# Two norms' gain and offset rows asked for at other moments in a mixture-of-experts decoder step

## Chip, cores and metric

The kernel runs on one core of a Trainium2 chip. The metric is the time of one execution on the device in microseconds (us). The engines are TensorE (PE, matrix products; PEld is its loading of stationary operands), VectorE (DVE), ScalarE (ACT), GpSimd (POOL) and SyncE (SP). SP and POOL each issue transfers from a queue of their own; the profile calls SP's queue q1 and POOL's q0.

## What is computed

One layer over 320 tokens of width 1024: 256 of one prompt and 64 of eight sampled sequences. In the reference's terms:

```python
mod = silu(c) @ w_ada + b_ada            # shift1, scale1, gate1, shift2, scale2, gate2
u = x * (1 + scale1) + shift1
proj = u @ w_in                          # conv branch, pooling branch, two gates
...
h = layer_norm(ALPHA * x + gate1 * (merged @ w_o), ln1_g, ln1_b)
v = h * (1 + scale2) + shift2
f = moe_ffn(v, ...)                      # each token goes to 4 of 32 experts
y = layer_norm(ALPHA * h + gate2 * f, ln2_g, ln2_b)

def expert_block(xb, e):                 # for each of the 32 experts
    h = xb @ w_up[e] + b_up[e]           # 1024 -> 2048
    glu, lin = min(h[:, :1024], 7), clip(h[:, 1024:], -7, 7)
    return (glu * sigmoid(1.702 * glu) * (lin + 1)) @ w_down[e] + b_down[e]
```

All is float32. An expert's weights are 12 MB in float32 (8 MB w_up, 4 MB w_down).

## The kernel before

Everything is written out by hand: each engine has one program, transfers are asked for in a fixed order, and engines wait on semaphores.

**The front.** SP loads weights in chunks of 2 MB into `ring`, which has six slots. The order is: a third of w_ada, the eight parts of w_in, a second third of w_ada, w_out_a, w_out_b, the last third of w_ada, and w_o (two chunks). The product with w_ada gives `mod`, which SP stores to DRAM in thirds (`store_mod`, L391) and reads back as rows copied to all partitions (`mod_for_tokens`, L419 and L421). With them SP loads the rows of the first norm into the ring (L424 and L425). The second third must be in DRAM before these loads are issued (L414). The last third is stored behind them, and when that has landed, scale2 is read back (L428, L429). VectorE waits for those rows, forms the residual and `v` per tile of 128 tokens in the order 0, 2, 1 (`residual`, `gain_and_offset`, `v_rows`). `v` feeds the router, the ranks of the tokens within each expert and the table of rounds.

**The expert loop.** A round handles up to 64 tokens of one expert, and an expert with more takes two rounds; here there are 35 rounds for 32 experts. TensorE does in a round: the up product (L870, four chunks c0 to c3 of 2 MB), small products that combine the last round's result into token order (L844), the gather of the next round's rows (L767), transposes of the activation (L895) and of the next rows (L776), and the down product (L904, four chunks m0 to m3 of 1 MB). Between up and down VectorE does the clamped product twice (`clamp`: L1345, L1346, L1348; `activate`: L1354) with ScalarE's sigmoid (L1035) in between; the transposes wait for both. SP asks for a chunk of the next expert (L437) when TensorE has done with the same chunk of the present one (`expert_used`, L454). SP's waits are in program order, so a late release of m0 holds up all that follows.

**POOL beside it.** POOL first prepares b_up (to L500), waits for the end of the output projection (`wait_full(pool, "o11")`, L502), and loads b_down. At the beginning of round 0 it subtracts parts of `v` (L517, six instructions). Then it asks for the rows of the first norm a second time, into `norm1_rows` (L520, L521), waits for them (L522), and makes the full h of three tiles with them, three instructions per tile (L527, L529, L531), in `hx`. h is used only in the tail. Then it asks for `tail_rows`: gate2 for the prompt (L534), gate2 for eight sequences (L536), ln2_g and ln2_b (L538, L539). After a wait for all of them (L543) POOL sleeps until the last round.

`norm1_rows` lies on the place of `b_up_rows`, which is free after L500. The ln2_g part of `tail_rows` lies on `V`, the ln2_b part on the first half of `norm1_rows`. ln1_g, ln1_b, ln2_g and ln2_b are 512 KB each when copied to 128 partitions.

**The tail.** After the last down product, the last result is combined, and each of three tiles is gated, added to h and normed. POOL multiplies tiles 0 and 1 by ln2_g (L558), adds ln2_b (L560) and stores them; VectorE does tile 2 (L1399, L1400).

Of the kernel before, what the change touches and what calls it, by code (L numbers as in the profile page):

```python
# [16 lines left out]
P = 128  # L17
D = 1024
# [3 lines left out]
NSEQ, TSEQ = 8, 8  # L22
# [6 lines left out]
E = 32  # L29
# [19 lines left out]
EXPERT_CHUNKS = UP_CHUNKS + DOWN_CHUNKS  # L49
# [33 lines left out]
def front_place(name):  # L83
    n = FRONT.index(name)
    return n % 8, n // 8
# [6 lines left out]
def program(nc, a, o):  # L92
    ctx = ExitStack()
    with ctx:
# [3 lines left out]
        def sem(name):  # L98
            return ctx.enter_context(nc.semaphore(name))
# [14 lines left out]
        def region(t, at, *shape):  # L114
            n = int(np.prod(shape))
            v = t[:, at:at + n]
            if len(shape) == 2:
                return v.rearrange("p (a b) -> p a b", a=shape[0])
            if len(shape) == 3:
                return v.rearrange("p (a b c) -> p a b c", a=shape[0], b=shape[1])  # L120
            return v
# [44 lines left out]
        tail_rows = region(front, 0, 4 * D)  # L166
# [7 lines left out]
        norm1_rows = region(front, 3072, 2, D)  # L174
# [58 lines left out]
        expert_landed = [sem(f"expert_landed{c}") for c in range(EXPERT_CHUNKS)]  # L233
# [7 lines left out]
        router_landed = sem("router_landed")  # L241
        norm1_landed = sem("norm1_landed")
        tail_landed = sem("tail_landed")
        bias_landed = sem("bias_landed")
        mod_stored = sem("mod_stored")
        out_stored = sem("out_stored")
# [22 lines left out]
        norm1_again = sem("norm1_again")  # L269
# [8 lines left out]
        b_up_ready = sem("b_up_ready")  # L278
# [63 lines left out]
        def wait_full(eng, name):  # L342
            b, n = front_place(name)
            eng.wait_ge(bank_full[b], n + 1)
            return bank[b]
# [113 lines left out]
        def _(pool):  # L459
# [39 lines left out]
                    part(pool.tensor_copy(parts, rows))  # L499
            pool.memset(b_up_rows[0:1, 0:1], 0.0).then_inc(b_up_ready, 1)  # L500

            wait_full(pool, "o11")  # L502
            for i in range(4):
                pool.dma_start(b_down_raw[32 * i:32 * i + E, :], a["b_down"][0][:, (i // 2) * 512:(i // 2 + 1) * 512]).then_inc(b_down_landed, 16)
# [11 lines left out]
                pool.wait_ge(v_part_ready, PARTS.index((t, q)) + 1)  # L516
                pool.tensor_tensor(V[0:r, t, :], V[0:r, t, :], v_parts[0:r, PART_AT[t][q], :], ALU.subtract).then_inc(v_rest_ready, 1)  # L517

            pool.wait_ge(b_up_ready, 1)
            pool.dma_start(norm1_rows[:, 0, :], a["ln1_g"][0].partition_broadcast(P)).then_inc(norm1_again, 16)  # L520
            pool.dma_start(norm1_rows[:, 1, :], a["ln1_b"][0].partition_broadcast(P)).then_inc(norm1_again, 16)  # L521
            pool.wait_ge(norm1_again, 32)  # L522
            for i, t in enumerate(TILE_ORDER):
                r = ROWS[t]
# [10 lines left out]
            for s in range(NSEQ):  # L535
                pool.dma_start(tail_rows[TSEQ * s:TSEQ * (s + 1), D:2 * D],  # L536
                               mod_rows[1 + s, 5 * D:].partition_broadcast(TSEQ)).then_inc(tail_landed, 16)
            pool.dma_start(tail_rows[:, 2 * D:3 * D], a["ln2_g"][0].partition_broadcast(P)).then_inc(tail_landed, 16)  # L538
            pool.dma_start(tail_rows[:, 3 * D:], a["ln2_b"][0].partition_broadcast(P)).then_inc(tail_landed, 16)  # L539

            pool.wait_ge(table_ready, 1)
            G = pool.value_load(table[0:1, 159:160], min_val=1, max_val=52)
            pool.wait_ge(tail_landed, 16 * (3 + NSEQ))  # L543
            pool.wait_ge(onehot_ready, G + 1)
            pool.wait_ge(bank_full[B_X], G + front_uses(B_X) + 1)
            for i, t in enumerate((1, 2)):
# [8 lines left out]
            for t in range(2):  # L555
                row = out_rows[:, t, :]
                pool.wait_ge(row_normed, 4 + t)
                pool.tensor_tensor(row, row, tail_rows[:, 2 * D:3 * D], ALU.mult).then_inc(h_step, 1)  # L558
                pool.wait_ge(h_step, 7 + 2 * t)
                pool.tensor_tensor(row, row, tail_rows[:, 3 * D:], ALU.add).then_inc(h_step, 1)  # L560
                pool.wait_ge(h_step, 8 + 2 * t)
                pool.dma_start(outs[t], row).then_inc(out_stored, 16)
# [489 lines left out]
        def _(dve):  # L1052
# [5 lines left out]
            def step(ins):  # L1058

                steps[0] += 1  # L1060
                ins.then_inc(step_sem[0], 1)
                dve.wait_ge(step_sem[0], origin[0] + steps[0])

            def signal(ins, sem, value):
                ins.then_inc(sem, 1)
                dve.wait_ge(sem, value)
# [108 lines left out]
            def normalise(r, meanwhile=lambda: None):  # L1175

                step(v.bn_aggr(aggr[0:r, :], stats[0:r, :]))
                normed[0] += 1
                signal(TS(aggr[0:r, 1:2], aggr[0:r, 1:2], EPS, None, ALU.add), var_ready, normed[0])
                meanwhile()  # L1180
                dve.wait_ge(sqrt_ready, normed[0])
                step(v.reciprocal(rstd[0:r, :], rstd[0:r, :]))

                step(STT(rstd2[0:r, :], rstd[0:r, :], rstd[0:r, :], aggr[0:r, 1:2], ALU.mult, ALU.mult))
                step(TS(rstd2[0:r, :], rstd2[0:r, :], -0.5, 1.5, ALU.mult, ALU.add))
                step(TT(rstd[0:r, :], rstd[0:r, :], rstd2[0:r, :], ALU.mult))
                signal(STT(shift[0:r, :], aggr[0:r, 0:1], -1.0, rstd[0:r, :], ALU.mult, ALU.mult), rstd_ready, normed[0])
# [184 lines left out]
                assert steps[0] == PER_LOOP  # L1372
            steps[0], origin[0], step_sem[0] = 0, 0, tail_step

            dve.wait_ge(tail_landed, 16 * (3 + NSEQ))
            dve.wait_ge(h_ready, 3)
            dve.wait_ge(bank_full[B_X], G + front_uses(B_X) + 1)
            gate2 = lambda t, h: tail_rows[0:ROWS[t], (0 if t < 2 else D) + h * 512:(0 if t < 2 else D) + (h + 1) * 512]
# [17 lines left out]
                    normalise(r)  # L1396

            r, row = ROWS[2], out_rows[0:ROWS[2], 2, :]
            normalise(r, meanwhile=lambda: step(STT(row, row, aggr[0:r, 0:1], tail_rows[0:r, 2 * D:3 * D], ALU.subtract, ALU.mult)))  # L1399
            signal(STT(row, row, rstd[0:r, :], tail_rows[0:r, 3 * D:], ALU.mult, ALU.add), y_ready, 1)  # L1400

# [41 lines left out]
```

## Time and profile before

| | |
|---|---|
| three runs | 1304.96, 1297.54, 1305.26 us (median 1304.96) |
| profiled execution | 1306.29 us, of which the span from first to last instruction 1304.5 us |
| mean granted TensorE clock | 0.966 of full speed |
| busy: PE, DVE, ACT, POOL | 1202.6, 550.4, 226.6, 160.6 us |
| DMA | 466.54 MB, mean 358 GB/s |
| expert weights | 128 issues of 2 MB and 128 of 1 MB |

Share of the 16 DMA engines and their rate in 40 slices of 32.6 us:

```profile
DMA  9744499649999999999996999998899999699951
GB/s 335 261 153 173 193 310 369 245 183 400 394 425 428 426 427 427 426 426 425 425 426 255 427 425 426 426 428 356 333 426 428 427 427 426 263 425 426 426 237 40
```

A digit is tenths of the slice, 9 being 90% or more. The expert loop begins in the ninth slice. TensorE is at 9 in nearly all slices as well, but its busy time includes matmuls drawn out behind weights that are arriving, so it does not say by itself which of the two sets the pace.

### The profile page before, as it was taken

The numbers are of one execution on the slowest core, as the hardware profiler recorded it, in microseconds if no ns is written. First come the engines' busy times: TensorE is split into PE (matmuls) and PEld (weight loads), VectorE is DVE, ScalarE is ACT, GpSimd is POOL, SyncE is SP. The second block draws the span as 40 slices with busy tenths as digits, with TensorE's granted clock in tenths as the row PEclk, the third lists the DMA queues.
The fourth block names the chain that finished last, engine by engine and source line by source line (L and its number), as shares of the span: only waits on it lengthen the run. The fifth ranks groups of instructions, "written<-read, shape, count | busy, mean of one in ns | idle before, by whom it ended". The sixth has DMA issues, their size and how long they took to land.

```text
span 1304.5 us, 17407 instructions
## 1 busy us (share of the span) xinstructions
PE 1202.6 (92%) x6170; PEld 520.2 (40%) x6171; DVE 550.4 (42%) x1044; ACT 226.6 (17%) x350; POOL 160.6 (12%) x97
## 2 busy tenths in 40 slices
PE   4899999979899999999899999999999999999990
PEld 0599964433333333333333333333333333333330
DVE  0517825874434333433334333443343433334337
ACT  0233210133112111111111111111111111111110
POOL 0367443024400000000000000000000000000023
PEclk8799999969899999999999999999999999999995
DMA  9744499649999999999996999998899999699951
GB/s 335 261 153 173 193 310 369 245 183 400 394 425 428 426 427 427 426 426 425 425 426 255 427 425 426 426 428 356 333 426 428 427 427 426 263 425 426 426 237 40
DMA packets 54789, 466.54 MB, mean 358 GB/s; under 512 B 5516, under 2 KB 5548, under 8 KB 18642
## 3 DMA queue, kind: packets, MB, share of 16 engines
q1 hardware_dynamic: 52817, 460.32, 85.9%
q0 software_dynamic: 1952, 5.97, 1.4%
q8 instruction: 12, 0.20, 0.1%
q14 instruction: 8, 0.06, 0.0%
HBM read 464.42 MB, written 1.85 MB: 357 GB/s over the span
## 4 chain that ended last, share of the span: by engine, by line
PE 60%; DMA 27%; DVE 9%; SPq 2%; ACT 1%; issue 1%; POOL 0%; DVEq 0%; ACTq 0%
PE bank L870 28%; DMA ring<-in_w_up 21%; PE bank L904 13%; PE bank L647 8%; PE bank L844 3%; DMA mod_rows<-parts_home 3%; DMA hx<-in_x_sample 2%; PE bank L767 2%; PE bank L633 2%; DVE front L1354 1%; PE bank L895 1%; ACT front L1038 1%; DVE front L1348 1%; PE bank L862 1%; DVE front L1345 1%
## 5 line engine op out<-in xcount | busy, mean ns | idle before, releaser
L870 PE MATMUL bank<-ring,front 128*64 128x512 f32 x2240 | 505.9, 597 | 20.3 <-DMA ring<-in_w_up 20.3
L870 PEld LDWEIGHTS bank<-ring,front 128*64 128x64 f32 x2240 | 153.5, 137 | 314.7 <-issue 269.8
L904 PE MATMUL bank<-ring,front 128*64 128x512 f32 x1120 | 250.2, 599 | 7.1 <-ACT front L1038 7.1
L1328 DVE TENSOR_TENSOR front<-front,bank 128x512 f32<-128x512 f32 (+1 forms) x210 | 143.7, 684 | 78.7 <-PE bank L844 65.9
L904 PEld LDWEIGHTS bank<-ring,front 128*64 128x64 f32 x1120 | 77.8, 138 | 155.5 <-issue 141.6
L1371 DVE TENSOR_TENSOR O_low<-bank,O_high 128x512 fp32r<-128x512 f32 x35 | 24.2, 691 | 247.0 <-ACT O_high L1041 247.0
L1035 ACT ACTIVATE front<-front 128x256 f32<-128x256 f32 x70 | 29.2, 417 | 529.0 <-DVE front L1345 529.0
L549 POOL TENSOR_TENSOR parts_home<-front 128x1024 f32<-128x1024 f32 (+1 forms) x2 | 4.7, 2356 | 919.9 <-DVE onehot_T L1368 919.9
L1345 DVE TENSOR_SCALAR front<-bank 128x256 f32<-128x256 f32 x70 | 29.7, 424 | 159.8 <-PE bank L870 158.6
L467 POOL TENSOR_TENSOR ring_parts<-ring,ring_parts 128x1024 fp32r<-128x1024 f32 x28 | 68.3, 2472 | 77.2 <-ACT ring_parts L937 77.2
L767 PE MATMUL bank<-parts_home,front 128*64 128x512 bf16 (+1 forms) x560 | 70.5, 382 | 0.0
L647 PE MATMUL bank<-u_high,ring_parts 128*128 128x320 f32 x448 | 67.1, 308 | 0.0
L844 PE MATMUL bank<-O_high,onehot_T 64*128 64x512 f32 x216 | 54.5, 501 | 13.5 <-DVE front L1390 11.7
L647 PEld LDWEIGHTS bank<-u_high,ring_parts 128*128 128x128 f32 x448 | 66.0, 188 | 0.0
L1041 ACT ACTIVATE O_high<-bank 128x512 fp32r<-128x512 f32 x35 | 20.9, 597 | 236.3 <-PE bank L904 236.3
L1268 DVE TENSOR_TENSOR front<-const,front 128x192 bf16 x35 | 14.8, 423 | 95.3 <-issue 95.3
L767 PEld LDWEIGHTS bank<-parts_home,front 128*64 128x64 bf16 (+1 forms) x560 | 32.3, 109 | 52.7 <-issue 35.3
L844 PEld LDWEIGHTS bank<-O_high,onehot_T 64*128 64x128 f32 x216 | 20.4, 185 | 80.2 <-issue 80.2
L1354 DVE SCALAR_TENSOR_TENSOR front<-front 128x256 f32<-128x256 f32 x70 | 49.8, 712 | 2.5
L1035 ACT ACT_TABLE_LOAD x35 | 44.9, 1283 | 0.6
L844 PE MATMUL bank<-O_low,onehot_T 64*128 64x512 f32 x216 | 43.1, 395 | 0.0
L605 PE MATMUL bank<-ring,small 128*9 128x512 f32 x192 | 27.7, 722 | 15.2 <-DMA ring<-in_w_ada 15.2
(217 smaller groups left out, 938.6 us busy)
## 6 DMA issues: line engine op xcount, KB each, us to landing
ring<-in_w_up SPq DMA_DIRECT2D x128, 2048.0 KB, 18.3
ring<-in_w_down SPq DMA_DIRECT2D x128, 1024.0 KB, 17.4
ring<-in_w_ada SPq DMA_DIRECT2D x12, 2048.0 KB, 16.0
ring<-in_w_in SPq DMA_DIRECT2D x8, 2048.0 KB, 11.9
ring<-in_w_o SPq DMA_DIRECT2D x2, 2048.0 KB, 19.6
hx<-in_x_prompt SPq DMA_DIRECT2D x2, 1024.0 KB, 23.7
ring<-in_w_out_a SPq DMA_DIRECT2D x1, 2048.0 KB, 7.3
ring<-in_w_out_b SPq DMA_DIRECT2D x1, 2048.0 KB, 14.2
```

Of the source, the lines that this page charges most:

```text
L467: pool.tensor_tensor(ring_parts[:, slot, part], ring[:, slot, part], ring_parts[:, HIGH_SLOT[i % 2], part].bitcast(F32), ALU.subtract).the ...
L605: last = mm(ps[32 * q:32 * q + NC_ROWS, :], sc_T[:, k, :], w[:, kk, q * 512:(q + 1) * 512], start=k == 0, stop=k == KC - 1)
L633: last = mm(blocks[j][:, 0:NT], w[:, k, j * P:(j + 1) * P], u_T[:, k, :], start=k == 0, stop=k == KC - 1)
L647: return mm(blocks[j][:, 0:NT], w[:, k, j * P:(j + 1) * P], u[:, k, :], start=start, stop=stop)
L767: last = mm(bank[B_X][64 * h:64 * h + 64, :], S[0:r, t, :], v_parts[0:r, at, h * 512:(h + 1) * 512], start=i == 0, stop=i == len(GATHER) - 1)
L844: last = mm(bank[B_C[h]][:, :], onehot_T[rows, t * P:(t + 1) * P], part[rows, :], start=not stop, stop=stop)
L870: last = mm(bank[B_UP[j]][64 * h:64 * h + 64, :], x_T[:, (c % 2) * 2 + b, 64 * (c // 2):64 * (c // 2) + 64], w[:, :, at:at + 256], start=F ...
L904: last = mm(bank[B_DOWN][64 * h:64 * h + 64, :], act_T[:, 2 * j + b, 64 * hh:64 * hh + 64], expert_chunk_at(UP_CHUNKS + m)[:, b * 1024 + h ...
L1035: AF(sig[:, j, :], glu[:, j, :], ACT.Sigmoid, scale=SWISH).then_inc(sig_ready, 1)
L1328: signal(TT(Y[0:r, 2 * t + h, :], Y[0:r, 2 * t + h, :], bank[b][0:r, :], ALU.add), bank_free[b], value)
L1345: signal(TS(glu[:, j, :], bank[b][:, 0:256], LIMIT, None, ALU.min), glu_ready, 2 * g + j + 1)
L1354: signal(STT(by_row, in_rows(lin), slot_gate, in_rows(sig), ALU.mult, ALU.mult), act_ready, 2 * g + j + 1)
```

## The change

The two loads of the first norm's rows into `norm1_rows` go from behind L517 to behind L500, ahead of POOL's wait for the output projection. Their wait (L522) stays where it was. The two loads of the last norm's rows go behind a new wait, for chunk m3 of the last expert. They signal a new semaphore `norm2_landed`. The two old waits for `tail_landed` count two loads less, and POOL (before its first L558) and VectorE (before the norm of tile 2) wait for `norm2_landed`.

```diff
--- before.py
+++ after.py
@@ -241,6 +241,7 @@
         router_landed = sem("router_landed")
         norm1_landed = sem("norm1_landed")
         tail_landed = sem("tail_landed")
+        norm2_landed = sem("norm2_landed")
         bias_landed = sem("bias_landed")
         mod_stored = sem("mod_stored")
         out_stored = sem("out_stored")
@@ -499,6 +500,9 @@
                     part(pool.tensor_copy(parts, rows))
             pool.memset(b_up_rows[0:1, 0:1], 0.0).then_inc(b_up_ready, 1)
 
+            pool.wait_ge(b_up_ready, 1)
+            pool.dma_start(norm1_rows[:, 0, :], a["ln1_g"][0].partition_broadcast(P)).then_inc(norm1_again, 16)
+            pool.dma_start(norm1_rows[:, 1, :], a["ln1_b"][0].partition_broadcast(P)).then_inc(norm1_again, 16)
             wait_full(pool, "o11")
             for i in range(4):
                 pool.dma_start(b_down_raw[32 * i:32 * i + E, :], a["b_down"][0][:, (i // 2) * 512:(i // 2 + 1) * 512]).then_inc(b_down_landed, 16)
@@ -516,9 +520,6 @@
                 pool.wait_ge(v_part_ready, PARTS.index((t, q)) + 1)
                 pool.tensor_tensor(V[0:r, t, :], V[0:r, t, :], v_parts[0:r, PART_AT[t][q], :], ALU.subtract).then_inc(v_rest_ready, 1)
 
-            pool.wait_ge(b_up_ready, 1)
-            pool.dma_start(norm1_rows[:, 0, :], a["ln1_g"][0].partition_broadcast(P)).then_inc(norm1_again, 16)
-            pool.dma_start(norm1_rows[:, 1, :], a["ln1_b"][0].partition_broadcast(P)).then_inc(norm1_again, 16)
             pool.wait_ge(norm1_again, 32)
             for i, t in enumerate(TILE_ORDER):
                 r = ROWS[t]
@@ -535,12 +536,13 @@
             for s in range(NSEQ):
                 pool.dma_start(tail_rows[TSEQ * s:TSEQ * (s + 1), D:2 * D],
                                mod_rows[1 + s, 5 * D:].partition_broadcast(TSEQ)).then_inc(tail_landed, 16)
-            pool.dma_start(tail_rows[:, 2 * D:3 * D], a["ln2_g"][0].partition_broadcast(P)).then_inc(tail_landed, 16)
-            pool.dma_start(tail_rows[:, 3 * D:], a["ln2_b"][0].partition_broadcast(P)).then_inc(tail_landed, 16)
 
             pool.wait_ge(table_ready, 1)
             G = pool.value_load(table[0:1, 159:160], min_val=1, max_val=52)
-            pool.wait_ge(tail_landed, 16 * (3 + NSEQ))
+            pool.wait_ge(tail_landed, 16 * (1 + NSEQ))
+            pool.wait_ge(expert_landed[EXPERT_CHUNKS - 1], 16 * E)
+            pool.dma_start(tail_rows[:, 2 * D:3 * D], a["ln2_g"][0].partition_broadcast(P)).then_inc(norm2_landed, 16)
+            pool.dma_start(tail_rows[:, 3 * D:], a["ln2_b"][0].partition_broadcast(P)).then_inc(norm2_landed, 16)
             pool.wait_ge(onehot_ready, G + 1)
             pool.wait_ge(bank_full[B_X], G + front_uses(B_X) + 1)
             for i, t in enumerate((1, 2)):
@@ -555,6 +557,8 @@
             for t in range(2):
                 row = out_rows[:, t, :]
                 pool.wait_ge(row_normed, 4 + t)
+                if t == 0:
+                    pool.wait_ge(norm2_landed, 32)
                 pool.tensor_tensor(row, row, tail_rows[:, 2 * D:3 * D], ALU.mult).then_inc(h_step, 1)
                 pool.wait_ge(h_step, 7 + 2 * t)
                 pool.tensor_tensor(row, row, tail_rows[:, 3 * D:], ALU.add).then_inc(h_step, 1)
@@ -1372,7 +1376,7 @@
                 assert steps[0] == PER_LOOP
             steps[0], origin[0], step_sem[0] = 0, 0, tail_step
 
-            dve.wait_ge(tail_landed, 16 * (3 + NSEQ))
+            dve.wait_ge(tail_landed, 16 * (1 + NSEQ))
             dve.wait_ge(h_ready, 3)
             dve.wait_ge(bank_full[B_X], G + front_uses(B_X) + 1)
             gate2 = lambda t, h: tail_rows[0:ROWS[t], (0 if t < 2 else D) + h * 512:(0 if t < 2 else D) + (h + 1) * 512]
@@ -1396,6 +1400,7 @@
                     normalise(r)
 
             r, row = ROWS[2], out_rows[0:ROWS[2], 2, :]
+            dve.wait_ge(norm2_landed, 32)
             normalise(r, meanwhile=lambda: step(STT(row, row, aggr[0:r, 0:1], tail_rows[0:r, 2 * D:3 * D], ALU.subtract, ALU.mult)))
             signal(STT(row, row, rstd[0:r, :], tail_rows[0:r, 3 * D:], ALU.mult, ALU.add), y_ready, 1)
```

## Rows read from the trace of the kernel before

**Rows 1.** The page: the chain of waits that ended last, by engine and by line.

```profile
PE 60%; DMA 27%; DVE 9%; SPq 2%; ACT 1%; issue 1%; POOL 0%; DVEq 0%; ACTq 0%
PE bank L870 28%; DMA ring<-in_w_up 21%; PE bank L904 13%; PE bank L647 8%; PE bank L844 3%; DMA mod_rows<-parts_home 3%; DMA hx<-in_x_sample 2%; PE bank L767 2%; PE bank L633 2%; DVE front L1354 1%; PE bank L895 1%; ACT front L1038 1%; DVE front L1348 1%; PE bank L862 1%; DVE front L1345 1%
```

**Rows 2.** The same chain in order of time: start, us, what.

```profile
216.09 14.36 DMA mod_rows<-parts_home
...
419.97 24.13 DMA ring<-in_w_up
...
654.62 25.65 DMA ring<-in_w_up
```

**Rows 3.** Stretches: us, busy PE, PEld, DVE, ACT, POOL, clock, DMA share, GB/s.

```profile
290.00:300.00 10.00, 10.00 (x50) 3.23 (x48) 4.94 (x8) 6.18 (x6) 10.00 (x6) 1.00 0.70 249
300.00:310.00 10.00, 9.73 (x58) 3.98 (x56) 5.82 (x12) 5.01 (x8) 2.20 (x3) 1.00 0.98 399
310.00:320.00 10.00, 10.00 (x52) 3.38 (x48) 1.18 (x2) 1.88 (x2) 1.29 (x1) 1.00 1.00 419
...
340.00:360.00 20.00, 20.00 (x87) 6.42 (x88) 5.19 (x11) 2.48 (x3) 3.09 (x7) 0.89 1.01 371
...
690.00:700.00 10.00, 10.00 (x52) 3.43 (x50) 1.49 (x3) 1.88 (x2) 0.00 (x0) 1.00 0.03 8
...
1257.00:1258.00 1.00, 1.00 (x8) 0.31 (x6) 0.93 (x3) 0.32 (x1) 0.00 (x0) 1.00 0.50 205
```

**Rows 4.** DMA between 209 and 224 us; then POOL's queue between 293 and 360.

```profile
DMA packets 1408, 5.98 MB, mean 399 GB/s; under 512 B 88, under 2 KB 88, under 8 KB 1268
...
q0 software_dynamic: 883, 2.57, 10.3%
```

**Rows 5.** POOL in order of time: start, us, line, operation, idle before.

```profile
208.72 0.09 POOL L500 MEMSET front<- 1x1 f32 x1
...
301.09 0.56 POOL L520 DMA_DIRECT2D front<-in_ln_g  x1
...
318.71 2.36 POOL L527 TENSOR_TENSOR hx<-hx,front 128x1024 f32<-128x1024 f32 x1 [16.51 <-DMA front<-in_ln_b]
...
330.75 2.36 POOL L527 TENSOR_TENSOR hx<-hx,front 128x1024 f32<-128x1024 f32 x1
```

**Rows 6.** VectorE in order of time, the clamped product of rounds 0 and 1.

```profile
303.60 0.43 DVE L1348 SCALAR_TENSOR_TENSOR front<-front 128x256 f32<-128x256 f32 x1
...
306.18 0.68 DVE L1354 SCALAR_TENSOR_TENSOR front<-front 128x256 f32<-128x256 f32 x1
...
330.77 2.62 DVE L1348 SCALAR_TENSOR_TENSOR front<-front 128x256 f32<-128x256 f32 x1
333.43 2.64 DVE L1354 SCALAR_TENSOR_TENSOR front<-front 128x256 f32<-128x256 f32 x1
```

**Rows 7.** TensorE in order of time, rounds 0 and 1.

```profile
308.26 7.09 PE L904 MATMUL bank<-ring,front 128*64 128x512 f32 x32 [0.21 <-ACT front L1038]
...
338.20 1.11 PE L895 MATMUL bank<-const,front 128*128 128x128 f32 x4 [4.18 <-DVE front L1354]
...
340.10 9.23 PE L904 MATMUL bank<-ring,front 128*64 128x512 f32 x32
```

**Rows 8.** SP's issues in order of time: start, us, what.

```profile
292.23 12.63 SPq L437 DMA_DIRECT2D ring<-in_w_up  x4
310.38 5.48 SPq L437 DMA_DIRECT2D ring<-in_w_down  x4
319.40 12.63 SPq L437 DMA_DIRECT2D ring<-in_w_up  x4
343.96 5.89 SPq L437 DMA_DIRECT2D ring<-in_w_down  x4
```

**Rows 9.** The tail, all engines in order of time.

```profile
1263.03 2.36 POOL L549 TENSOR_TENSOR parts_home<-front 128x1024 f32<-128x1024 f32 x1 [919.94 <-DVE onehot_T L1368]
...
1282.75 2.39 POOL L558 TENSOR_TENSOR parts_home<-parts_home,front 128x1024 f32<-128x1024 f32 x1 [10.19 <-ACT parts_home L969]
```

## The prediction

> **What bounds the kernel now.** The chain of waits comes first [rows 1]. It ends in TensorE for 60% and in DMA for 27%, nearly all of the latter w_up. So the loop has two limits that take turns. The same chain in order of time shows where [rows 2]. From the loop's start to 420 us it runs along TensorE alone. From 419.97 to 680 us it runs through one w_up transfer per round, nine in all, the last of 25.65 us. After that it is mostly TensorE again. There is one such transfer ahead of the loop that matters too: the store of the last third of `mod`, 14.36 us.
>
> The stretches say what the chain can't [rows 3]. DMA is busy without a gap from 293 us on: 0.98 at 300 to 310, 1.00 at 310 to 320, and so in all slices to 680 us. It first stands still at 690 to 700 us (0.03), when an expert takes two rounds. So TensorE lives on chunks loaded ahead up to 444 us, but the moment at which it gets past 680 us was set by the transfers queued since 293 us. A byte taken out of this stream counts, even one at 301 us where TensorE waits for nothing; a gap put into it counts just as much. After 690 us both follow the shift that they had at 680.
>
> **The change part by part.** Experts are numbered from 0, so the first stream is expert 1's.
>
> *The two ln1 loads leave the stream.* They are issued at 301.09 [rows 5] and are 1.05 MB. POOL's queue moved 2.57 MB in 10.3% of 67 us, 6.9 us [rows 4], so 1.05 MB cost 2.8 us. The lower bound is 2.5 us at 419 GB/s. The upper one takes them for the cause of the slowest stretch, 371 instead of 419 GB/s from 340 to 360 us [rows 3]: that is 0.96 MB less, 2.3 us, so 4.8 in all. I take -2.8, as the queue's own rate is the nearest row.
>
> *The two ln2 loads leave the stream.* Same size, same bounds, and they do lie just before that slow stretch. I take -2.8, at most -4.8. Together the two give 5.6.
>
> *The two ln1 loads arrive at 208.8.* POOL is free there since its last memset [rows 5]; b_up_ready is its own signal and costs nothing. But this is not an empty place. Between 209 and 224 us DMA moves 399 GB/s [rows 4] for w_o, for SP's own copies of the ln1 rows and for the rows of `mod`, and behind them waits the store that is on the chain from 216.09 to 230.45 [rows 2]. VectorE's first residual and then scale2 wait for just these, and from there VectorE's serial chain leads to the table and to the loop. 1.05 MB at 399 GB/s are 2.6 us of delay. From below: before, the pair on POOL's queue landed only at 318.7 after an issue at 301.65 [rows 5], 1.05 MB in 17 us or 62 GB/s beside SP's queue. At that pace 0.9 MB come through up to 223 us and the rest falls behind, where the engines are half idle: 2.0 us. Nothing excludes 0 if all of it slid there. From above: 4.8, as for the slow stretch. I take +2.6, as the nearest row is that of the stretch itself.
>
> The Trainium skill, DMA: Bandwidth & Descriptors, section "Queues, rings and completion order", states that each DMA engine takes turns between the queues it has work for, a packet at a time. By that rule the POOL loads can't wait behind SP's, which speaks against this half of the change: the head's term would be the full 2.6, and 0 would be excluded. The trace before agrees in part: the pair did land while SP's queue was full, but only after 17 us, so the turns were not equal in bytes.
>
> *POOL's work on h moves.* Its wait for the rows was 16.51 us [rows 5]. It disappears, so L527 begins behind L517 at 301.1 and the nine instructions end at 319, not 337. In round 1 these had collided with VectorE: L1348 took 2.62 us beside POOL's L527 at 330.75, against 0.43 in round 0, and L1354 2.64 against 0.68 [rows 5, 6]. Each held until POOL's instruction ended. Then TensorE stood idle 4.18 us, and L904 took 9.23 instead of 7.09, the granted clock being 0.89 from 340 to 360 us [rows 3, 7]. Now the same nine meet round 0. On the old time axis L529 runs 303.5 to 305.9, L531 to 307.0, L527 to 309.5, L529 to 312.0. L1348 at 303.60 is held to 306.2; L1354 and two instructions that were not held before follow up to 307.9; the second L1348 is held to 309.8, the second L1354 to 312.3. Without POOL it ended at 306.86 [rows 6]: TensorE waits 5.4 us. Round 1, which lasted 34.0 us between the first L870 and the next against 27.2 in undisturbed rounds, is freed of these 6.8 us and round 0 gets about 8. For TensorE alone that cancels, and up to 444 us its time is not the bound.
>
> For the stream it does not cancel. SP asks for m0 of expert 1 when TensorE has read m0 of expert 0: 310.38 [rows 8], 2.1 us into L904. In the slowed round 1, L904 began 2.0 instead of 1.4 us after the last L1354, and m0 was asked for 3.9 instead of 2.1 us into it [rows 7, 8]. So now it is asked for at 310.38 + 5.4 + 0.6 + 1.7 = 318.1, and with the head's delay at 320.7. What has DMA until then? The four w_up chunks, 8.39 MB, plus ln1, 1.05 MB. 2.49 + 3.99 MB are moved by 310 [rows 3], and the remaining 2.96 MB at 419 GB/s last to 317.1. Before, there were 6.7 us of work in the queue when m0 was asked for at 310.38. Without ln1 the work ends at 314.3, with the head's delay at 316.9. From the issue at 320.7 the data take about 1.4 us (between 0.8 and 1.9, from 292.23 to the first bytes and to a full rate). So DMA stands idle from 316.9 to 322.1: **5.2 us**. A second gap is covered: m0 to m3 last 10 us, to 332.1, with gate2's rows behind them, and c0 of expert 2 is asked for at 319.40 + 2.6 + 8.1 = 330.1 [rows 8]. The bounds are 0, if POOL's instructions don't hold VectorE there, and 7.
>
> *The ln2 loads at the end.* The last chunk has landed by about 1257.7, where DMA falls to half [rows 3]. POOL is asleep until 1263.03 and first uses the rows at 1282.75, 25 us later [rows 9]; VectorE later still. Two issues of 0.56 us and 2.8 us of transfer are covered by that wait: 0. Without the cover they would cost 4 to 5 us. The two added waits for `norm2_landed` are already met. What is queued behind POOL's new wait is only the tail, which it slept through anyway.
>
> **The sum.** +2.6 + 5.2 - 2.8 - 2.8 = +2.2 us. On the profiled execution's 1306.29 us that gives 1308.5. That execution lies 1.3 us above the median of the runs, so I forecast **1307 us**, against 1304.96. A measurement of this kernel can tell about 1% from no change, 13 us; its own three runs lie 7.7 us apart.
>
> **The rivals.** *A, the stream does not run dry.* POOL's work on h meets VectorE less than I have it, or m0 comes early enough; then the 5.2 fall to 0 and the saved bytes stay saved: +2.6 - 5.6 = -3.0, 1302. With a head that costs nothing and ln2 at its 4.8 it is -7.6, 1297. For it: my 6.7 us of queue are worked out from rates of 10 us stretches, and a collision depends on fractions of a microsecond. Against: nine instructions without a gap can't miss a product of four.
>
> *B, slower, the clock.* TensorE stood idle 4.18 us in round 1 and lost 2.1 us in L904 behind it. Behind 5.4 us the clock may stay at the lower of its two levels, 1.2 GHz, for all of L904: twice 7.09, 14.2 instead of 9.2 us. Then m0 comes 1.5 us later, and each of the three chunks behind it is released every 3.5 us where DMA needs 2.5, so it waits 1 us for each. That is +2.2 + 4.5 = +6.7, and with the head at 4.8 +8.9: 1312 to 1314. It becomes a loss over 1% only where the gap reaches 5.2 + 10.8 = 16 us. Against it: in round 1 the idle time was nearly as long, and L904 took 9.23, so the clock came back within it.
>
> *C, the change does nothing of the kind*: the ln rows were never in the way because TensorE, not DMA, sets 680 us. Then the head's 2.6 and the difference of the rounds are left, 5.4 + 0.6 + 2.1 = 8.1 in round 0 less 6.8 in round 1: +3.9, 1309. Rows 2 speak against it.
>
> **How the numbers follow.** Forecast 0.45, A 0.33, B 0.10, C 0.07, others 0.05. The range covers the forecast (1303 to 1311 with its bounds), A and B: 1297 to 1313. That holds 0.95 by the cases; I take off what the scatter of the runs may put outside, and am left with 0.8. No case with the prices above leaves the 1%. I give faster by over 1% 0.03 (before's fastest run, 1297.54, with A gets near 1292), slower by over 1% 0.04 (B with a larger gap), within 1% 0.93.
>
> **What would show it.** In the profile of the changed kernel: the wait of VectorE for the rows of `mod` ends near 232, not 229.7; the loop's first L870 starts 2.6 us later. POOL's L527 starts right behind L517. The long L1348 and L1354 are in round 0, and TensorE's wait of about 5 us for L1354 stands there and not in round 1. DMA shows a gap of some 5 us near 317 to 322. The w_up transfer that ends near 680 ends near 682. At the end two loads stand at 1258 to 1263 and no wait for them. Signs against me would be: no gap in DMA near 320 (then A), a round 0 longer than 38 us (then B), or TensorE waiting for the rows in the tail.

## The result, and the profile after

The changed kernel takes **1308.34 us** (median of 20 runs, 1306.20 to 1311.63) where the kernel before takes 1304.83 (20 runs, 1297.54 to 1309.00). The ratio is 1.003, with a 95% interval of 1.0021 to 1.0040: 2.7 to 5.2 us slower. The forecast was 1307 us, 2.2 above before.

Lines have other numbers in the changed kernel. TensorE's L870 is now L874, L895 is L899 and L904 is L908. VectorE's L1348 and L1354 are L1352 and L1358. POOL's L527, L529 and L531 are L528, L530 and L532, its L558 is L562, and SP's L437 is L438. In ln1_half they are as before; in the other experiments they are up to two higher than in the changed kernel.

The chain of waits in order of time (start, us, what) answers to [rows 2]:

```profile
216.93 14.16 DMA mod_rows<-parts_home
231.11 4.13 DMA ring<-mod_rows
...
449.13 25.64 DMA ring<-in_w_up
...
655.78 25.62 DMA ring<-in_w_up
```

The chain is of the same kind, with eight w_up transfers where before had nine. The last one before DMA's first rest ends at 681.40, 1.1 us later than before's 680.27. DMA sets the time from 449 and not from 420 us on. That fits the start of round 2, which is 1.8 us later on TensorE (351.43 against 349.60) where the stream is 1.1 us later, but no run shows that this is the reason.

The stretches (busy PE, PEld, DVE, ACT, POOL, then granted clock, DMA share, GB/s) answer to [rows 3]:

```profile
290.00:300.00 10.00, 10.00 (x48) 3.17 (x46) 4.94 (x8) 5.28 (x5) 10.00 (x5) 0.95 0.58 210
300.00:310.00 10.00, 8.00 (x46) 2.83 (x42) 5.97 (x7) 4.67 (x6) 9.74 (x6) 1.00 1.00 416
310.00:320.00 10.00, 6.27 (x22) 2.95 (x24) 6.71 (x6) 1.24 (x3) 9.58 (x6) 0.66 0.50 213
320.00:330.00 10.00, 10.00 (x52) 3.37 (x50) 2.31 (x4) 1.88 (x2) 5.07 (x10) 1.00 0.99 357
```

At 310 to 320 us DMA is busy for half the time, where before it was at 1.00. Finer, at each end of the gap:

```profile
314.00:315.00 1.00, 1.00 (x6) 1.00 (x6) 0.88 (x2) 0.12 (x1) 0.92 (x2) 0.50 0.89 377
315.00:316.00 1.00, 1.00 (x6) 0.59 (x6) 0.96 (x2) 0.74 (x2) 1.00 (x1) 0.50 0.16 66
316.00:317.00 1.00, 1.00 (x4) 0.24 (x2) 0.97 (x2) 0.33 (x1) 0.92 (x2) 0.50 0.00 0
...
319.00:320.00 1.00, 1.00 (x6) 0.28 (x4) 0.00 (x0) 0.00 (x0) 0.91 (x2) 1.00 0.00 0
320.00:321.00 1.00, 1.00 (x8) 0.41 (x6) 0.00 (x0) 0.00 (x0) 0.46 (x1) 1.00 0.88 188
```

From about 315.2 to 320.2 nothing moves. The granted clock is at the lower level (0.50) from about 311.5 to 318.3; TensorE had been idle since 308.0, and the clock came back within L908. What made the gap is on three engines. POOL (start, us; it answers to [rows 5]):

```profile
302.22 2.35 POOL L528 TENSOR_TENSOR hx<-hx,front 128x1024 f32<-128x1024 f32 x1
304.65 2.36 POOL L530 TENSOR_TENSOR hx<-hx,front 128x1024 f32<-128x1024 f32 x1
307.11 1.10 POOL L532 TENSOR_SCALAR hx<-hx 128x1024 f32<-128x1024 f32 x1
308.28 2.45 POOL L528 TENSOR_TENSOR hx<-hx,front 64x1024 f32<-64x1024 f32 x1
310.81 2.40 POOL L530 TENSOR_TENSOR hx<-hx,front 64x1024 f32<-64x1024 f32 x1
```

VectorE beside it [rows 6], and TensorE behind it [rows 7]:

```profile
304.74 2.55 DVE L1352 SCALAR_TENSOR_TENSOR front<-front 128x256 f32<-128x256 f32 x1
307.32 1.33 DVE L1358 SCALAR_TENSOR_TENSOR front<-front 128x256 f32<-128x256 f32 x1
...
309.60 1.42 DVE L1352 SCALAR_TENSOR_TENSOR front<-front 128x256 f32<-128x256 f32 x1
311.05 2.62 DVE L1358 SCALAR_TENSOR_TENSOR front<-front 128x256 f32<-128x256 f32 x1
```

```profile
313.73 1.11 PE L899 MATMUL bank<-const,front 128*128 128x128 f32 x4 [5.73 <-DVE front L1358]
...
315.63 8.41 PE L908 MATMUL bank<-ring,front 128*64 128x512 f32 x32
```

Each of VectorE's four instructions ends just behind one of POOL's: 307.29 behind 307.01, 308.65 behind 308.21, 311.02 behind 310.73, 313.67 behind 313.21. TensorE waits 5.73 us for the last. SP then asks for m0 (the first issue of `in_w_down` here) at 319.06 and not at 310.38 [rows 8]:

```profile
293.37 12.63 SPq L438 DMA_DIRECT2D ring<-in_w_up  x4
319.06 5.48 SPq L438 DMA_DIRECT2D ring<-in_w_down  x4
328.09 12.62 SPq L438 DMA_DIRECT2D ring<-in_w_up  x4
```

The tail [rows 9] has the two loads ahead of POOL's gating, and no engine waits for them:

```profile
1261.43 0.55 POOL L544 DMA_DIRECT2D front<-in_ln_g  x1 [935.79 <-DMA ring<-in_w_down]
...
1264.75 2.36 POOL L551 TENSOR_TENSOR parts_home<-front 128x1024 f32<-128x1024 f32 x1 [2.25 <-DVE onehot_T L1372]
...
1284.46 2.40 POOL L562 TENSOR_TENSOR parts_home<-parts_home,front 128x1024 f32<-128x1024 f32 x1 [10.19 <-ACT parts_home L973]
```

### The profile page after: what moved, and what is told of

The parts are those of the page before. It is cut to its first block, busy times and chain, and to the rows that moved or that the text cites. A ratio compares the mean times of both kernels' runs of the same rounds, so it can differ in the third digit from the quotient of the medians.

```text
span 1306.2 us, 17410 instructions
## 1 busy us (share of the span) xinstructions
PE 1201.9 (92%) x6170; PEld 518.7 (40%) x6171; DVE 558.9 (43%) x1044; ACT 226.5 (17%) x350; POOL 160.6 (12%) x97
## 3 DMA queue, kind: packets, MB, share of 16 engines
HBM read 464.42 MB, written 1.85 MB: 357 GB/s over the span
## 4 chain that ended last, share of the span: by engine, by line
PE 64%; DMA 26%; DVE 7%; ACT 1%; issue 1%; SPq 1%; POOL 0%; DVEq 0%; ACTq 0%
PE bank L874 29%; DMA ring<-in_w_up 20%; PE bank L908 14%; PE bank L651 8%; PE bank L848 4%; PE bank L771 3%; DMA ring<-in_w_ada 3%; DMA hx<-in_x_sample 2%; PE bank L637 1%; PE bank L899 1%; ACT front L1042 1%; DMA mod_rows<-parts_home 1%; PE bank L866 1%; PE bank L609 1%; PE bank L833 1%
## 5 line engine op out<-in xcount | busy, mean ns | idle before, releaser
L874 PE MATMUL bank<-ring,front 128*64 128x512 f32 x2240 | 506.1, 597 | 20.1 <-DMA ring<-in_w_up 20.0
L874 PEld LDWEIGHTS bank<-ring,front 128*64 128x64 f32 x2240 | 153.3, 137 | 314.8 <-issue 269.2
L908 PE MATMUL bank<-ring,front 128*64 128x512 f32 x1120 | 249.4, 598 | 7.0 <-ACT front L1042 7.0
L908 PEld LDWEIGHTS bank<-ring,front 128*64 128x64 f32 x1120 | 77.6, 137 | 154.8 <-issue 140.9
L1358 DVE SCALAR_TENSOR_TENSOR front<-front 128x256 f32<-128x256 f32 x70 | 50.3, 719 | 2.5
## 6 DMA issues: line engine op xcount, KB each, us to landing
ring<-in_w_down SPq DMA_DIRECT2D x128, 1024.0 KB, 17.6
```

The lines of the kernel that those rows point to most:

```text
L874: last = mm(bank[B_UP[j]][64 * h:64 * h + 64, :], x_T[:, (c % 2) * 2 + b, 64 * (c // 2):64 * (c // 2) + 64], w[:, :, at:at + 256], start=F ...
L908: last = mm(bank[B_DOWN][64 * h:64 * h + 64, :], act_T[:, 2 * j + b, 64 * hh:64 * hh + 64], expert_chunk_at(UP_CHUNKS + m)[:, b * 1024 + h ...
L1358: signal(STT(by_row, in_rows(lin), slot_gate, in_rows(sig), ALU.mult, ALU.mult), act_ready, 2 * g + j + 1)
```

## Experiments

Every kernel was measured against the kernel before, and each row of the table has one trace. The scatter of a kernel's runs (some 5 us) is larger than most of the terms. The traces split the time into parts, of which the stream and the rest scatter less: in the three kernels that were traced twice, the stream differs by 0.1 to 1.7 us and the rest by 0.3 to 1.3 us. A difference of 1 us between two streams therefore says nothing. The table below is worked out from the traces. "Loop starts" is the start of the first up product. "Stream" is from there to the end of the w_up transfer near 680 us, the last on the chain before DMA's first rest. "Rest" is from there to the issue of the last store. "Against before" is by the ratio of the runs, in us with its 95% interval.

| kernel | loop starts | stream | rest | against before |
|---|---|---|---|---|
| before | 287.04 | 393.2 | 618.4 | |
| changed | 288.14 | 393.3 | 618.9 | +3.9 (2.7 to 5.2) |
| changed_again | 286.01 | 392.7 | 619.8 | +3.0 (1.3 to 4.7) |
| ln1_half | 287.86 | 395.4 | 619.7 | +4.2 (2.2 to 6.1) |
| ln2_half | 286.07 | 390.1 | 619.2 | -3.1 (-4.8 to -1.3) |
| h_held | 287.43 | 387.8 | 618.7 | -3.9 (-5.7 to -2.2) |
| ln1_in_idle_dma | 286.13 | 388.6 | 619.0 | -6.1 (-8.2 to -3.9) |
| ln1_in_idle_dma_again | 285.43 | 386.9 | 618.8 | -5.1 (-6.9 to -3.4) |
| h_round0_no_head | 286.58 | 392.8 | 619.6 | +1.3 (-0.1 to 2.7) |
| h_round0_no_head_again | 285.25 | 392.9 | 618.3 | +1.4 (-0.3 to 3.1) |
| h_in_round_9 | 288.88 | 388.0 | 620.3 | -4.6 (-6.1 to -3.1) |
| all_tail_rows_last | 284.40 | 383.1 | 622.4 | -6.1 (-7.8 to -4.6) |
| gate_rows_beside_last_down | 284.56 | 383.3 | 620.2 | -6.5 (-8.2 to -4.8) |

**The changed kernel beside the others.**

> The changed kernel itself, beside the others. My theory: the stream of expert weights sets the time at 680 us. The head costs +1.3 us (the trace after shows the loop starting 1.1 us later), DMA stands idle for 5.1 us in round 0, the four loads taken out give back 5.6 us: about +1 to +2 us, with the 20 runs so far at +3.5. Rival 'head': the gap is covered by chunks loaded ahead and costs nothing, and what the change costs lies before the loop. Rival 'TensorE': TensorE sets the time, the loads were never in the way, and what is left is that round 0 loses more than round 1 gains. All three have to give this kernel's +2 to +4 us.

Measured: 1308.42 us against 1304.56. Its loop started at 286.01, 2 us sooner than in the first trace, and the stream took the same 393 us. So the start of the loop scatters by itself, and a head term can't be read from it in one trace. The +3.0 (1.3 to 4.7) lies above the +1 to +2 that my theory gave.

In this trace and the four others with the gap, what DMA's share is short of 1.00, summed over the slices of 1 us about the gap, is 4.8 to 5.4 us.

**The ln1 loads alone.** The lines on ln2 are as before. Against the kernel before:

```diff
 # POOL
+            pool.wait_ge(b_up_ready, 1)
+            pool.dma_start(norm1_rows[:, 0, :], ...)      # ln1_g
+            pool.dma_start(norm1_rows[:, 1, :], ...)      # ln1_b
             wait_full(pool, "o11")
 ...
-            pool.wait_ge(b_up_ready, 1)                   # behind L517
-            pool.dma_start(norm1_rows[:, 0, :], ...)
-            pool.dma_start(norm1_rows[:, 1, :], ...)
             pool.wait_ge(norm1_again, 32)
```

> Only the ln1 loads are moved; the ln2 loads stay in the stream behind gate2's rows. My theory: the changed kernel plus the 2.8 us of the ln2 loads, so 2 to 4 us above the changed kernel and about +4 to +6 us against before. Rival 'TensorE': equal to the changed kernel. Rival 'head': the stream matters there too, so the same as my theory; this run does not tell those two apart.

Measured: 1310.47, 2.05 us above the changed kernel's median. Its stream of 395.4 is 2.4 longer than the changed kernel's (mean of two, 393.0). That fits the ln2 pair. "TensorE sets the time" asked for no difference; the intervals of the two kernels overlap, so this run alone doesn't settle it.

**The ln2 loads alone.** Against the changed kernel:

```diff
-            pool.wait_ge(b_up_ready, 1)                   # not ahead of "o11"
-            pool.dma_start(norm1_rows[:, 0, :], ...)
-            pool.dma_start(norm1_rows[:, 1, :], ...)
 ...
+            pool.wait_ge(b_up_ready, 1)                   # behind L517, as before
+            pool.dma_start(norm1_rows[:, 0, :], ...)
+            pool.dma_start(norm1_rows[:, 1, :], ...)
             pool.wait_ge(norm1_again, 32)
```

> Only the ln2 loads are moved; the ln1 loads and POOL's work on h stay where they were. My theory: nothing in the head, no gap, 1.05 MB less in the stream: -2.8 us against before (-2.5 to -4.8). Its trace should show the w_up transfer that ends at 680 us end 3 us earlier, round 1 as slow as before, and the tail unchanged with the two loads behind the last chunk. Rival 'TensorE': 0.

Measured: 1302.85 against 1304.56; the stream is 3.2 us shorter than before's, ending at 650.49 + 25.64:

```profile
650.49 25.64 DMA ring<-in_w_up
```

This half of the change is a gain of 3.1 us by the runs (1.3 to 4.8), where 2.8 was forecast and "TensorE" asked for 0. The loss is in the other half.

**POOL's work held back to round 1.** Against the changed kernel:

```diff
+            pool.wait_ge(O_low_ready, 2)
             pool.wait_ge(norm1_again, 32)
```

> The changed kernel, but POOL's work on h waits until VectorE has the low part of round 0's result (about 317 us), so that it meets VectorE in round 1, as before, and not in round 0. The ln1 loads stay early. My theory: the gap of 5.1 us in DMA goes, and the time falls by about 5 us against the changed kernel, to -2 to -4 us against before; the trace shows DMA without a gap at 315 to 321 us. Rival 'head': equal to the changed kernel. Rival 'TensorE': equal to the changed kernel within 1 us, since one slow round takes the place of another.

Measured: 1301.64, 6.8 us below the changed kernel on the same chip. One added wait on POOL turns the loss into a gain. The gap is nearly gone (clock 0.84, DMA share 0.88 here, against 0.66 and 0.50 in the changed kernel), where I had expected none of it; some 1.3 us are left at 313 to 316 us. In this trace VectorE waited 2.08 us for ScalarE, with POOL idle, and TensorE 1.85 us for VectorE; its down product then began at the lower clock and took 8.68 us and not 7.09:

```profile
310.00:320.00 10.00, 9.98 (x42) 3.34 (x44) 1.39 (x3) 1.69 (x3) 0.00 (x0) 0.84 0.88 328
```

```profile
308.68 0.65 PE L900 MATMUL bank<-const,front 128*128 128x128 f32 x4 [1.85 <-DVE front L1359]
...
310.02 8.68 PE L909 MATMUL bank<-ring,front 128*64 128x512 f32 x32 [0.21 <-ACT front L1043]
```

The rival "head", by which the gap is covered, and the rival "TensorE" both wanted no change. Both fall. That one slow round only took the place of another holds for TensorE: rounds 0 and 1, from the first up product of round 0 to that of round 2, last 62.4 us here and 63.3 and 63.1 us in the two traces of the changed kernel, 0.6 to 0.9 us more, while the stream differs by 5.2.

**The ln1 loads where DMA rests.** As h_held, and against it:

```diff
-            pool.wait_ge(b_up_ready, 1)                   # ahead of "o11"
-            pool.dma_start(norm1_rows[:, 0, :], ...)
-            pool.dma_start(norm1_rows[:, 1, :], ...)
             wait_full(pool, "o11")
 ...
             pool.memset(Y, 0.0).then_inc(cleared, 1)
+            pool.wait_ge(b_up_ready, 1)
+            pool.dma_start(norm1_rows[:, 0, :], ...)
+            pool.dma_start(norm1_rows[:, 1, :], ...)
```

> As h_held, with the ln1 loads issued not at 209 us but behind POOL's clearing of Y at about 280 us, where the trace of before shows DMA at a share of 0.01 (280 to 290). My theory: the head's term, +1.3 us by the trace after (2.6 as predicted), goes: 1 to 3 us below h_held, -4 to -6 us against before. The loads land within 5 us and nothing waits for them. Rival 'the early loads are free in the head': equal to h_held.

> The same kernel as ln1_in_idle_dma, to narrow the size of the gap's cost against the next one: -4 to -6.5 us against before.

Measured: 1299.69 and 1298.65, so -6.1 and -5.1 against before, where h_held had -3.9. The loads landed in 4.7 us, against 17 us for the pair before. DMA is at 1.00 from 310 to 320 us. The intervals of this kernel and h_held overlap, so these runs alone do not show the head's term; the traces do, below.

**The gap without the head.** The changed kernel with the ln1 loads behind the clearing of Y, POOL's work not held.

> The changed kernel with the ln1 loads behind the clearing of Y (about 280 us), and POOL's work on h not held, so in round 0 as in the changed kernel. It has the gap without the head's term. My theory: 1 to 3 us below the changed kernel, so between 0 and +2 us against before, and 5 us above ln1_in_idle_dma. Rival 'head': the same as ln1_in_idle_dma.

> The same kernel as h_round0_no_head. By the gap in its trace (DMA at rest from about 313.5 to 318.5 us) it should be 5 us above ln1_in_idle_dma_again; the first runs had 7.1 between the medians. If the gap is all, the difference is 4 to 6; if something else is lost as well, 6 to 8.

Measured: +1.3 and +1.4 against before, 7.1 and 6.4 us above ln1_in_idle_dma in the two sets of runs. The streams differ by 5.1 (392.8 against a mean of 387.8). The half in DMA's share at 310 to 320 us is there again:

```profile
310.00:320.00 10.00, 8.90 (x36) 3.88 (x38) 4.12 (x5) 1.19 (x2) 9.11 (x8) 0.75 0.50 195
```

Moving 1 MB of loads to an idle place did not close the gap while POOL's work stood in round 0: the gap comes from when POOL works. By what I had written down for the second set, 6.4 would mean that something is lost beside the gap. The 1.6 us between the mean of 6.7 and 5.1 I can't place; no part of the traces shows it, and the intervals leave room for nothing beside the gap.

**POOL's work held until round 9's result.** Against ln1_in_idle_dma:

```diff
-            pool.wait_ge(O_low_ready, 2)
+            pool.wait_ge(O_low_ready, 11)
```

> As ln1_in_idle_dma, with POOL's work on h held until VectorE has round 9's result (about 560 us), where TensorE waits for weights in every round. gate2's rows are asked for behind it, at 580 us, still in the stream. My theory: the slow round costs nothing while DMA sets the time, wherever it is, so equal to ln1_in_idle_dma within 1.5 us. Rival 'TensorE': TensorE's lost 3 to 7 us in round 1 count, and this is 3 to 7 us below ln1_in_idle_dma.

Measured: -4.6, no different from ln1_in_idle_dma, with a stream of 388.0. The work now stands beside round 10, and there it met VectorE much less: TensorE waited 1.06 us and its down product took the undisturbed 7.09:

```profile
591.69 0.66 PE L900 MATMUL bank<-const,front 128*128 128x128 f32 x4 [1.06 <-DVE front L1359]
...
593.04 7.09 PE L909 MATMUL bank<-ring,front 128*64 128x512 f32 x32 [0.21 <-ACT front L1043]
```

So this run doesn't put a slow round elsewhere; it takes one away. Nor was the one taken away as long as the rival had it: round 1 of ln1_in_idle_dma lasts 29.4 us against 27.1 undisturbed, 2.3 us lost and not 3 to 7. Taken over three kernels the rival still fails. Rounds 0 and 1 last 62.4 us in h_held, 59.1 and 59.6 in the two traces of ln1_in_idle_dma and 56.8 here, 5.6 us less than in h_held, and the four streams lie between 386.9 and 388.6, this one at 388.0. TensorE's loss in round 1 costs nothing; a delay in round 0 that leaves DMA without work costs its gap.

Gate2's rows move along with the work, and here their price can be read from the chain, where the transfers around it last 25.65:

```profile
558.77 25.66 DMA ring<-in_w_up
588.30 29.57 DMA ring<-in_w_up
```

The second is 3.9 us longer, for 0.79 MB.

**All the tail's rows last.** As h_in_round_9, with gate2's loads behind the wait for the last chunk and POOL's `tail_landed` wait behind `onehot_ready` (the lines that these leave are not shown):

```diff
+            pool.wait_ge(expert_landed[EXPERT_CHUNKS - 1], 16 * E)
             pool.dma_start(tail_rows[:, 0:D], ...)        # gate2, prompt
             for s in range(NSEQ): ...                     # gate2, eight sequences
             pool.dma_start(tail_rows[:, 2 * D:3 * D], ...)
             pool.dma_start(tail_rows[:, 3 * D:], ...)
             pool.wait_ge(onehot_ready, G + 1)
+            pool.wait_ge(tail_landed, 16 * (1 + NSEQ))
```

> As h_in_round_9, with gate2's rows (0.79 MB in nine transfers) also asked for behind the last expert's last chunk, ahead of the ln2 rows. My theory: the stream loses another 0.79 MB at 327 to 419 GB/s, 1.9 to 2.4 us: -6 to -9 us against before, the fastest of all. POOL's nine issues of 0.5 us lie before its first use at about 1263 us, so the tail may start up to 2 us late on POOL, which has 10 us of idle time before it is needed. Rival 'the tail is hit': the gain of 2 us is lost to it.

Measured: -6.1. The stream lost 4.9 us, twice what I expected for the bytes. But the tail was hit, as the rival had it: from the last down product's start to the last store it took 39.88 us, before 36.62. POOL issued its eleven loads from 1248.30 on, waited 0.96 us for gate2's rows and began its gating at 1255.02, so that the rest of it met VectorE's:

```profile
1258.93 4.17 DVE L1385 TENSOR_TENSOR parts_home<-front 128x512 f32<-128x512 f32 x2 [0.36 <-DVE O_low L1376]
1263.14 3.24 DVE L1386 TENSOR_TENSOR parts_home<-parts_home,hx 128x1024 f32<-128x1024 f32 x1
```

Before, the same two took 2.94 and 1.23 us:

```profile
1270.89 2.94 DVE L1380 TENSOR_TENSOR parts_home<-front 128x512 f32<-128x512 f32 x2 [0.36 <-DVE O_low L1371]
1273.87 1.23 DVE L1381 TENSOR_TENSOR parts_home<-parts_home,hx 128x1024 f32<-128x1024 f32 x1
```

**Gate2's rows a little earlier.** Against all_tail_rows_last:

```diff
-            pool.wait_ge(expert_landed[EXPERT_CHUNKS - 1], 16 * E)
+            pool.wait_ge(expert_landed[UP_CHUNKS - 1], 16 * E)
             ...                                           # gate2's nine loads
+            pool.wait_ge(expert_landed[EXPERT_CHUNKS - 1], 16 * E)
             ...                                           # the two ln2 loads
```

> As all_tail_rows_last, with gate2's rows asked for when the last expert's last w_up chunk (c3) has landed, beside its four w_down chunks; the ln2 rows stay behind m3. In all_tail_rows_last the stream to 668 us was 5 us shorter than in h_in_round_9, but POOL's last instructions then met VectorE's in the tail (L1385 and L1386: 4.17 + 3.24 us where before had 2.94 + 1.23). My theory: the last w_down chunk lands up to 5 us later, at about 1257 us, and is needed at about 1262; POOL's gating starts in time, the tail takes its old length, and the time falls by 3 us against all_tail_rows_last, to -7 to -10 us against before. Rival 'the last chunks are late': TensorE waits for m1 to m3, and the gain is lost.

Measured: 1297.30 us, the lowest median of all, -6.5 against before (-8.2 to -4.8). That misses the -7 to -10 that I expected, and the 3 us against all_tail_rows_last didn't show (-6.5 against -6.1). TensorE waited for none of the last chunks, and the tail has most of its old length back, 37.52 us by the same measure:

```profile
1259.37 3.83 DVE L1386 TENSOR_TENSOR parts_home<-front 128x512 f32<-128x512 f32 x2 [0.36 <-DVE O_low L1377]
1263.23 1.23 DVE L1387 TENSOR_TENSOR parts_home<-parts_home,hx 128x1024 f32<-128x1024 f32 x1
```

Its interval overlaps with those of all_tail_rows_last and ln1_in_idle_dma, so that it beats them isn't shown; that it beats before and the changed kernel is.

## Why the prediction was right

*The loads that leave the stream, -2.8 each.* Measured: 3.2 for the ln2 pair (393.2 less 390.1) and, with both pairs out and little or no gap in between, 5.4 together (393.2 less 387.8, the mean of h_held, ln1_in_idle_dma twice and h_in_round_9). Forecast 5.6. Both figures stand on the one trace of before.

*POOL's work meets round 0.* It began right behind L517 (302.22). VectorE's product ended at 313.67; the forecast for it was 312.3 on the old time axis and the loop started 1.1 us later, so 313.4. One detail was wrong: I let the first L1354 run unhindered beside POOL's L531, but POOL's tensor_scalar held it too (1.33 us against 0.68). It changed nothing, as the next instruction waited for the same L528 either way. TensorE waited 5.73 us where 5.4 was forecast, and its down product took 8.41, less than round 1's 9.23. Round 0 lasted 36.2 us instead of 28.6, 7.6 more where about 8 was forecast, and round 1 27.1 instead of 34.0.

*The gap, +5.2.* m0 was asked for at 319.06, 25.7 us behind c0's 293.37; the forecast was 318.1 less 292.23, 25.9. DMA stood still from about 315.2 to 320.2, 5.0 us. The streams give it from another side: 393.0 in the changed kernel against 387.8 with the same bytes and no gap, 5.2; a size of this kind is good to about 1 us. Rival A, a stream that doesn't run dry, is what h_held made; it did not happen by itself. Rival B needed the lower clock through all of L904; it held for about 2.7 of L908's 8.41 us (315.6 to 318.3). Rival C, that TensorE sets the time, fell with ln2_half and h_held.

*The head, +2.6.* This was mis-sized. It can be measured between SP's issue of its own ln1_g load, behind the store of the second third, and the landing of the last third's store. With POOL's loads in between this took 21.6, 22.5, 21.8 and 21.7 us in four traces, 21.9 on average. Without them it took 19.1 to 20.8 us in nine traces, 20.0 on average. So the term is about 2.0 us (21.91 less 19.95). The runs fit that: the kernels with the early loads are 1.6 to 2.6 us (+3.9 and +3.0 against +1.3 and +1.4) and 1.2 to 2.2 us (-3.9 against -6.1 and -5.1) behind their partners without, each difference with an interval wider than itself. The signs that I named for 2.6 came out smaller too: VectorE's wait for the rows ended at 230.37 and not near 232, and the loop began 1.1 us later.

I took all the bytes at the rate of the stretch. The rest of that chain is not at full rate in any case (from 223 us on DMA's share is under 0.8 before), so some of the delay may have fallen into it; no run shows that by itself. My lower value happened to be 2.0, but its working doesn't hold: 0.9 MB at 399 GB/s are 2.3 us, and POOL's loads landed within 8.4 and 10.5 us, not at the pace of 17. The rule on turns between the queues, from the Trainium skill's page DMA: Bandwidth & Descriptors, section "Queues, rings and completion order", fits the landing better than the 62 GB/s that I read from the old place. By it the loads come through among SP's, and they did (q0 with 1.05 MB in this stretch, 17.6% of it). The full 2.6 that I had drawn from it is not what was measured.

```profile
q1 hardware_dynamic: 1252, 5.12, 85.0%
q0 software_dynamic: 288, 1.05, 17.6%
```

*The tail, 0.* From the last down product's start to the last store it took 36.61 us, before 36.62. I had counted the cover from where DMA's share falls, 1257.7; in the changed kernel it falls at about 1259.3, and POOL's wait for the last chunk ended only at 1261.43, so the cover was 23 us and not 25. That cost nothing.

*The sum.* 2.0 + 5.2 - 5.4 = +1.8 us by the parts, +2.2 as forecast, +2.7 to +5.2 by the first 20 runs and +1.3 to +4.7 by the 12 of the second set. The parts come out at the low end of what the runs give, and the forecast below the first interval. Part of that may be the profiled execution of before, which lies 1.5 us above the median of its 20 runs: its stream may be longer than the usual one, and then the 5.4 is too large. The remaining 1 to 2 us I leave open; both kernels with POOL's work in round 0 have them.

## What to carry to other kernels

Where two limits take turns, ask of a moved piece not only which of them it is on but whether the other one still has work queued: here DMA had 6.7 us of work queued when m0 was asked for, 2.8 of them for 1 MB that TensorE never waited for. Taking that away together with a shift of POOL's work into round 0 opened a gap of 5 us that no later round gave back. When a wait is removed, look at what the freed engine will now run beside; POOL's nine instructions cost nothing beside rounds 1 and 10 and 5 us beside round 0. A place where DMA rests (280 to 290 us here) was worth more for a load than an earlier place in a full queue, ahead of a store that the chain waits for.

## What the runs showed that was not expected

Gate2's rows are dear: 0.79 MB in one load of 512 KB and eight of 32 KB to eight partitions each cost 3.9 us where they could be read from the chain, and 4.9 by the streams (388.0 less 383.1), where their bytes at 419 GB/s are 1.9. Which of the nine is the dear one, no run shows. The ln1 and ln2 pairs, 1.05 MB each to all 128 partitions, cost 2.7 on average. So the slow stretch that I charged to the ln2 loads as a bound belongs to gate2's rows, as far as the traces tell: it is there in the changed kernel too, at 320 to 330 us with a share of 0.99 and 357 GB/s, when the ln2 loads are gone.

A single-input tensor_scalar of POOL held a two-input instruction of VectorE as its tensor_tensor does (1.33 us against 0.68), while VectorE's own tensor_scalar instructions (one source, in a bank) kept their 0.42 us beside POOL's tensor_tensor.

How much the same nine instructions of POOL cost TensorE depends on where they fall in a round: round 1 was longer by 6.8 us before, by 3.8 in h_held and by 2.3 in ln1_in_idle_dma.
